# First loads of a two-layer decoder step reordered: x in quarters, params by GpSimd, first norm from row sums

## The chip, the core and the metric

The kernel runs as one launch on one core of a Trainium2 chip. The metric is device time in microseconds (us), the median of the runs. The engines are TensorE (PE in the rows; its weight loads are PEld), VectorE (DVE), ScalarE (ACT), GpSimd (POOL) and SyncE (SP); SP issues most of the DMAs, GpSimd and ScalarE can issue some too.

## What is computed

One inference step of a two-layer decoder trunk, in float32: 512 prompt rows and 8 x 4 sample rows of width 1024, so T = 544 rows together. The part that the change touches is the head of layer A:

```
h = rms(x, norm_mix[0])               # x * rsqrt(mean(x*x) + 1e-6) * gain
a, g, mq = split(h @ w_in_a[0], [768, 1536])
c, st = causal_dwconv(a * sigmoid(g), conv_a_prev, conv_a_w, conv_a_b)   # 31 taps
...
m = mem_attend(rms(mq), mem_k, mem_v)
x = x + concat([silu(layernorm(c)), m]) @ w_out_a
```

Behind it come a gated feed-forward part, a layer with differential attention over shared and paged keys and values, and a second feed-forward part. Twelve arrays are returned: the two results, and new states and caches.

## The kernel before, in words

Everything in the model's width is kept turned: channels on the 128 partitions, rows along the free axis. The residual `x_resid` is 128 x 8 x 544, eight chunks of 128 channels. Each engine has its own written-out program, and semaphores alone tie them together, so the order of every queue is the order of the code.

A product with a weight is a row of steps; one step is one block of 128 output channels. SP loads its slice of 512 KB (`w_raw`, four slots, `load`, L408). ScalarE rounds it to `w_hi` (`split_hi`, L990), VectorE makes the rest `w_lo` (`split_lo`, L1378), and the input is split in the same way into `xa_hi` (ScalarE, `scaled_hi`, L1020) and `xa_lo` (VectorE, `scaled_lo`, L1414), both with the norm's gain worked in. TensorE then runs, for each of the eight chunks k, hi times hi, lo times hi and hi times lo, each as two matmuls of 272 columns into two banks of `acc` (`mm_step`, L473): 48 matmuls a step. The norm's per-row factor `rstd` is multiplied in when VectorE takes the step's result out of `acc` (`from_acc`, L1446).

Steps 0 and 1 make the first 128 channels of a and of g (`glu_a`, `glu_g`). Before them stands the setup:

- SP (L390): constants, the x sample, the left half of x's columns, 16 loads of parameter rows and 4 small ones, the right half of x, then weight slices 0 and 1, conv states, FFN states, lambdas, memory rows, and the next slices.
- TensorE turns x and the parameter rows against an identity into two banks of `psT` in turn (L533 to L553), parameters between chunk 3 and chunk 4; VectorE copies each bank out (L1420 to L1429).
- ScalarE splits both weight slices and then, chunk by chunk, squares x (`square`, L1003) and makes `xa_hi`. GpSimd adds the squares up (`add_squares`, L2000), and there are two buffers of squares between them. TensorE sums over partitions with a matrix of ones after step 0 (`model_square_sum`, L501), VectorE turns, and takes the root with ScalarE (`root`, L1390), into `rstd`.
- Then a small part for the lambdas and the rest `tap_lo` of the conv's taps, `glu_a`, `glu_g`. Behind step 1 TensorE turns the memory rows and the states, sums their squares and goes on with step 2.

Of the conv's 31 taps ten a channel chunk run on TensorE as matmuls with diagonal matrices (`conv_unit`, L605), the others on VectorE.

Of the kernel before, what the change touches and what calls it, by code (L numbers as in the profile page):

```python
# [86 lines left out]
def build(nc, a):  # L87
    ctx = ExitStack()
    with ctx:
        def sem(name):  # L90
            return ctx.enter_context(nc.semaphore(name))
# [45 lines left out]
        small, _ = place("small", [P, 3, H * T // 32])  # L137
        lamt, _ = place("lam", [P, 8])
# [27 lines left out]
        frow, e1 = place("ffn_state_rows", [2 * 2 * DB, FF], at=e1)  # L166
        sprod, e2 = place("sample_tap_products", [P, DB, DS, TAPS], at=w0 + 12 * T)
# [59 lines left out]
        ld_x = [sem(f"ld_x{i}") for i in range(2)]  # L227
# [88 lines left out]
        SQ = dict(n0=0, mem=8, tA=16, ln=22, n1=28, n2=36, tB=44, n3=58)  # L316
        RT = dict(n0=0, mem=1, ln=2, n1=3, n2=4, n3=5)

        PARAMS_AT = KD // 2
# [44 lines left out]
        def tap_sum(j):  # L364
            return (psT, psX)[j % 2][:, :, 0:NPR // 2]
# [25 lines left out]
        def _(sp):  # L391
            sp.dma_start(cst[:, :], a["consts"]).then_inc(ld_const, 16)
            x_rows = a["x_prompt"].rearrange("o (i p) n -> (o p) i n", p=P)
            sp.dma_start(xnat[0:NSA, QB, :], a["x_sample"].rearrange("b t n -> (b t) n")).then_inc(ld_x[0], 16)
            sp.dma_start(xnat[:, 0:QB, 0:512], x_rows[:, :, 0:512]).then_inc(ld_x[0], 16)
            for r, k, src, done in put:
                if src is not None:
                    sp.dma_start(rows[r % P:r % P + k, r // P, :], src[done:done + k, :]).then_inc(ld_rows, 16)  # L398
                    continue
            for name in ("mem_q", "mem_k"):  # L400
                r = col[name]
                assert r // P == (r + 1) // P
                for h in range(2):
                    sp.dma_start(rows[r % P:r % P + 2, r // P, h * MHD:(h + 1) * MHD],
                                 a[name + "_norm"]).then_inc(ld_rows, 16)
            sp.dma_start(xnat[:, 0:QB, 512:D], x_rows[:, :, 512:D]).then_inc(ld_x[1], 16)
# [14 lines left out]
            for s in range(S_IN, S_MEM):  # L421
                m = s // 2 + CC * (s % 2) if s < 2 * CC else s
                load(s, block_cols(win, m))
                if s == 1:
                    sp.dma_start(crow[0:120, :, :], a["state_conv_a"][0].rearrange("(g b) t n -> (b t) g n", g=2)
                                 ).then_inc(ld_state, 16)
                    sp.dma_start(frow[:, :], a["state_ffn_conv"].rearrange("l b r n -> (l b r) n")).then_inc(ld_state, 16)
                    sp.dma_start(lamin[:, :, :].rearrange("p c n -> p (c n)"),
                                 a["lambdas"].rearrange("o c n -> o (c n)").partition_broadcast(P)).then_inc(ld_lam, 16)
# [42 lines left out]
        def _(pe):  # L472
# [62 lines left out]
            pe.wait_ge(ld_x[0], 32)  # L535
            b = setup_bank(0)
            for c in range(KD):
                last = nc.tensor.transpose(b[:, c * NSA:(c + 1) * NSA], xnat[0:NSA, QB, c * P:(c + 1) * P],
                                           ident[0:NSA, 0:NSA])
            last.then_inc(setup_filled, 1)  # L540
            for c in range(KD):
                if c == PARAMS_AT:
                    pe.wait_ge(ld_rows, 16 * (sum(1 for x in put if x[2] is not None) + 4))
                    b = setup_bank(1 + c)
# [4 lines left out]
                    pe.wait_ge(ld_x[1], 16)  # L549
                b = setup_bank(1 + c + (c >= PARAMS_AT))  # L550
# [1609 lines left out]
```

## Time and profile before

| | us |
|---|---|
| median of 3 runs | 1599.25 |
| lowest and highest run | 1593.43, 1603.15 |
| span of the profiled execution | 1595.4 |
| PE busy (matmul) | 1467.6 (92%) |
| DVE busy | 959.0 (60%) |
| ACT busy | 577.3 (36%) |
| POOL busy | 119.7 (8%) |

The page gives no time of the profiled execution beside its span. A busy PE is one with matmuls under way, pipelined, so 92% is no measure of how near it is to its peak. What a stretch costs is read from the chain of waits and from the timeline of that stretch, and not from shares of the whole span.

### The profile page before, as it was taken

The numbers are of one execution on the slowest core, as the hardware profiler recorded it, in microseconds if no ns is written. First come the engines' busy times: TensorE is split into PE (matmuls) and PEld (weight loads), VectorE is DVE, ScalarE is ACT, GpSimd is POOL, SyncE is SP. The second block draws the span as 40 slices with busy tenths as digits, with TensorE's granted clock in tenths as the row PEclk, the third lists the DMA queues.
The fourth block names the chain that finished last, engine by engine and source line by source line (L and its number), as shares of the span: only waits on it lengthen the run. The fifth ranks groups of instructions, "written<-read, shape, count | busy, mean of one in ns | idle before, by whom it ended". The sixth has DMA issues, their size and how long they took to land.

```text
span 1595.4 us, 27270 instructions
## 1 busy us (share of the span) xinstructions
PE 1467.6 (92%) x10820; PEld 1393.1 (87%) x10820; DVE 959.0 (60%) x1827; ACT 577.3 (36%) x949; POOL 119.7 (8%) x133
## 2 busy tenths in 40 slices
PE   4899867899999999999999996888999999999997
PEld 3799765789999999999888884765999999999997
DVE  4789888556663664466767775217366635653662
ACT  3444434444431222223445554125243322221232
POOL 2000103210000000001100003211010000000001
PEclk8899997789999999999999998998899999999999
DMA  7121222122233233222322224431123233233222
GB/s 208 42 65 54 93 79 81 30 66 82 85 87 93 85 87 93 81 85 74 91 73 60 68 65 167 165 104 53 40 80 93 80 92 93 80 93 88 85 74 67
DMA packets 208538, 134.87 MB, mean 85 GB/s; under 512 B 4971, under 2 KB 201152, under 8 KB 208391
## 3 DMA queue, kind: packets, MB, share of 16 engines
q1 hardware_dynamic: 201319, 105.30, 23.0%
q0 software_dynamic: 7120, 28.18, 5.4%
q8 instruction: 71, 1.16, 0.3%
q14 instruction: 28, 0.23, 0.0%
HBM read 126.24 MB, written 7.85 MB: 84 GB/s over the span
## 4 chain that ended last, share of the span: by engine, by line
PE 72%; DVE 17%; ACT 5%; issue 3%; DMA 1%; SPq 1%; POOL 0%; POOLq 0%; ACTq 0%; DVEq 0%
PE acc L485 55%; PE acc L662 6%; DVE conv_out L1478 3%; ACT w_hi L999 2%; PE acc L963 2%; DVE w_lo L1385 2%; PE psX L751 1%; PE psX L946 1%; DVE softmax_stats L1864 1%; ACT exps L1288 1%; DVE turned L1402 1%; DVE root_row L1411 1%; PE psT L696 1%; SPq L398 1%; PE psX L844 1%
## 5 line engine op out<-in xcount | busy, mean ns | idle before, releaser
L485 PE MATMUL acc<-xa_hi,w_hi 128*128 128x272 f32 x1824 | 384.8, 292 | 10.6 <-DVE xa_lo L1416 10.1
L485 PE MATMUL acc<-xa_hi,w_lo 128*128 128x272 f32 x1824 | 378.7, 289 | 0.0
L485 PE MATMUL acc<-xa_lo,w_hi 128*128 128x272 f32 x1824 | 377.6, 289 | 0.0
L999 ACT ACTIVATE w_hi<-w_raw 128x1024 fp32r<-128x1024 f32 x194 | 205.4, 1059 | 383.1 <-PE acc L485 306.5
L485 PEld LDWEIGHTS acc<-xa_hi,w_hi 128*128 128x128 f32 x1824 | 289.1, 189 | 13.1 <-issue 10.2
L1385 DVE TENSOR_TENSOR w_lo<-w_raw,w_hi 128x1024 fp32r<-128x1024 f32 x194 | 237.6, 1225 | 84.8 <-ACT w_hi L999 83.2
L485 PEld LDWEIGHTS acc<-xa_lo,w_hi 128*128 128x128 f32 x1824 | 288.3, 190 | 0.0
L485 PEld LDWEIGHTS acc<-xa_hi,w_lo 128*128 128x128 f32 x1824 | 286.2, 190 | 0.0
L485 PE MATMUL acc<-xb_hi,w_hi 128*128 128x272 f32 x832 | 174.8, 291 | 2.0 <-DVE xb_lo L1812 2.0
L485 PE MATMUL acc<-xb_hi,w_lo 128*128 128x272 f32 x832 | 172.1, 288 | 0.0
L485 PE MATMUL acc<-xb_lo,w_hi 128*128 128x272 f32 x832 | 171.6, 288 | 0.0
L1749 DVE TENSOR_TENSOR x_resid<-acc,x_resid 128x544 f32<-128x544 f32 (+1 forms) x64 | 46.4, 724 | 170.8 <-PE acc L485 139.9
L485 PEld LDWEIGHTS acc<-xb_hi,w_hi 128*128 128x128 f32 x832 | 130.6, 188 | 3.1 <-DVE xb_lo L1812 2.4
L485 PEld LDWEIGHTS acc<-xb_lo,w_hi 128*128 128x128 f32 x832 | 130.7, 188 | 0.0
L485 PEld LDWEIGHTS acc<-xb_hi,w_lo 128*128 128x128 f32 x832 | 129.9, 189 | 0.0
L1478 DVE SCALAR_TENSOR_TENSOR conv_out<-glu_ext,params,conv_out 128x512 f32<-128x512 f32 x120 | 86.2, 772 | 0.4
L1219 ACT ACTIVATE gelu<-gate_conv,params 128x544 f32<-128x544 f32 x44 | 33.0, 751 | 133.6 <-DVE gate_conv L1792 133.5
L1792 DVE SCALAR_TENSOR_TENSOR gate_conv<-gate_ext,params,gate_conv 128x512 f32<-128x512 f32 (+1 forms) x176 | 78.7, 497 | 0.1
L1803 DVE TENSOR_TENSOR value<-acc,rstd 128x544 f32<-128x544 f32 x44 | 31.9, 724 | 53.9 <-PE acc L485 53.9
L662 PE MATMUL acc<-xb_hi,w_hi 128*128 128x272 f32 x256 | 57.1, 306 | 7.6 <-DVE xb_lo L1741 5.7
L1223 ACT ACTIVATE xb_hi<-product 128x544 f32 x44 | 29.0, 658 | 89.1 <-DVE product L1809 89.1
L1812 DVE TENSOR_TENSOR xb_lo<-product,xb_hi 128x544 f32 (+1 forms) x44 | 31.9, 726 | 40.5 <-ACT xb_hi L1223 40.5
(298 smaller groups left out, 1989.3 us busy)
## 6 DMA issues: line engine op xcount, KB each, us to landing
w_raw<-in_w_up SPq DMA_DIRECT2D x88, 512.0 KB, 3.9
w_raw<-in_w_down SPq DMA_DIRECT2D x32, 512.0 KB, 3.9
w_raw<-in_w_in_a SPq DMA_DIRECT2D x14, 512.0 KB, 4.3
w_raw<-in_w_down SPq DMA_DIRECT2D x16, 384.0 KB, 3.3
w_raw<-in_w_kv SPq DMA_DIRECT2D x12, 512.0 KB, 3.8
k_pages<-in_cache_k POOLq DMA_DIRECT2D x16, 384.0 KB, 4.3
v_pages<-in_cache_v POOLq DMA_DIRECT2D x16, 384.0 KB, 3.9
w_raw<-in_w_mem_kv SPq DMA_DIRECT2D x8, 512.0 KB, 3.9
```

Source lines behind the costliest of these rows:

```text
L485: last = nc.tensor.matmul(acc[slot][:, c, 0:n], w, x[:, k, c * n:(c + 1) * n], start=(k == 0 and q == 0), stop=(k == kb - 1 and q == 2))
L662: last = nc.tensor.matmul(acc[s % 2][:, c, 0:HT], w, x[:, k, c * HT:(c + 1) * HT], start=(i == 0 and q == 0), stop=(i == KD - 1 and q == 2))
L963: last = nc.tensor.matmul(o_rows(h), apad[:, b2, pg, h, :], vpg[:, b2, pg, h * VD:(h + 1) * VD], start=(g + b2 + pg == 0 and h % 4 == 0), ...
L999: nc.scalar.activation(whi[:, slot % 2, :], wraw[:, slot, :], ACT.Copy).then_inc(w_hi_ready, 1)
L1219: nc.scalar.activation(gel[:, :], gcv[:, :], ACT.Gelu_apprx_tanh, bias=pcol_at("ffn_conv_b", q)).then_inc(gelu_ready, 1)
L1223: nc.scalar.activation(xb_hi[:, bass.ds(i * 2 + cc, 1), :].rearrange("p o n -> p (o n)"), prod[:, :], ACT.Copy).then_inc(uhi_ready, 1)
L1385: nc.vector.tensor_tensor(wlo[:, slot % 2, :], wraw[:, slot, :], whi[:, slot % 2, :].bitcast(F32), ALU.subtract).then_inc(w_lo_ready, 1)
L1478: ins = nc.vector.scalar_tensor_tensor(out=o, in0=src, scalar=w, in1=o, op0=ALU.mult, op1=ALU.add)
L1749: nc.vector.tensor_tensor(x, acc[b_][:, :, 0:HT], x, ALU.add).then_inc(acc_free, 1)
L1792: ins = nc.vector.scalar_tensor_tensor(out=o, in0=x, scalar=w, in1=o, op0=ALU.mult, op1=ALU.add)
L1803: nc.vector.tensor_tensor(val[:, :].rearrange("p (c n) -> p c n", c=2), acc[(sc + 1) % 2][:, :, 0:HT], rstd[:, :].rearrange("p (c n) -> p ...
L1812: nc.vector.tensor_tensor(lo, prod[:, :], hi.bitcast(F32), ALU.subtract).then_inc(ulo_ready, 1)
```

## The change

- SP loads only the identity's 128 columns of the constants first, then the x sample, the first quarter of x's columns, weight slice 0, the other three quarters of x, weight slice 1, and the other constants after that.
- GpSimd issues the parameter rows and the lambdas, ahead of its page table load and of its copy of the conv state from DRAM to DRAM.
- ScalarE issues one small load of the first norm's gains (`gain_rows`), which TensorE turns first of all.
- TensorE turns only the x sample and chunks 0 and 1 ahead of step 0; chunk k + 2 is turned between the matmuls of step 0, just before those of chunk k. The parameter rows are turned inside step 1, after chunk 5.
- VectorE's copies of chunks stand between its `xa_lo`, and ScalarE makes `xa_hi` as soon as a chunk is there.
- The first norm no longer comes from squares of the turned x that GpSimd adds. ScalarE squares the rows as loaded (128 rows x 1024, four and a short one) and sums along the row; VectorE makes variance, reciprocal root and five diagonal matrices, and TensorE multiplies ones by them, which spreads `rstd` over the partitions.
- A tap matmul on TensorE takes 512 columns into one bank, where there were two of 256 into two banks.

The core of the diff:

```diff
-            sp.dma_start(cst[:, :], a["consts"]).then_inc(ld_const, 16)
+            sp.dma_start(cst[:, 0:C_BLK], a["consts"][:, 0:C_BLK]).then_inc(ld_const, 16)
...
+            load_x(0)
...
                 load(s, block_cols(win, m))
+                if s == 0:
+                    for q in range(1, 4):
+                        load_x(q)
...
+            def x_arrives(k):
+                if k + 2 < KD:
+                    turn_x(k + 2)
+                pe.wait_ge(xg_lo, k + 1)
+
+            turn_x(0)
+            turn_x(1)
+            mm_step(0, 0, xa_hi, xa_lo, ready=x_arrives)
...
-            model_square_sum("n0")
-            mm_step(1, 1, xa_hi, xa_lo)
+            mm_step(1, 1, xa_hi, xa_lo, hooks=params_in)
+            for i in range(QB):
+                pe.wait_ge(n0_diag, i + 1)
+                nc.tensor.matmul(psX[:, 0, i * P:(i + 1) * P], ones[:, :], qf[:, 0, i * P:(i + 1) * P], start=True, stop=True)
...
-                    for c in range(2):
-                        at = PE_TAPS[i] + c * (NPR // 2)
-                        last = nc.tensor.matmul(tap_sum(j)[:, c, :], diag[:, u % 2, d, :], x[:, at:at + NPR // 2],
-                                                start=(i + q == 0), stop=(i == NPT - 1 and q == 2))
+                    last = nc.tensor.matmul(tap_sum(j), diag[:, u % 2, d, :], x[:, PE_TAPS[i]:PE_TAPS[i] + NPR],
+                                            start=(i + q == 0), stop=(i == NPT - 1 and q == 2))
...
+            act.dma_start(grow[:, :], a["norm_mix"].rearrange("l (c p) -> (l c) p", p=P)).then_inc(ld_gain, 16)
+            for c in range(KD):
+                act.wait_ge(setup_drained, c + 3)
+                scaled_hi(xa_hi, c, xT[:, c, :], pcol("norm_mix", c), xg_hi)
+                if c == 1:
+                    split_hi(0)
             split_hi(1)
-            for c in range(KD):
-                act.wait_ge(setup_drained, c + 2 + (c >= PARAMS_AT))
-                square(xT[:, c, :])
...
+                nc.scalar.activation(sqt[0:n, :, :].rearrange("p c n -> p (c n)")[:, 0:D], xnat[0:n, i, :], ACT.Square,
+                                     accum_out=rowsum[0:n, i:i + 1]).then_inc(n0_sum, 1)
...
+            for c in range(KD + 1):
+                if c < KD:
+                    dve.wait_ge(setup_filled, c + 3)
+                    nc.vector.tensor_copy(xT[:, c, 0:NPR], psT[:, c % 2, :]).then_inc(setup_drained, 1)
+                if c:
+                    scaled_lo(xa_lo, xa_hi, c - 1, xT[:, c - 1, :], pcol("norm_mix", c - 1), xg_hi, xg_lo, c)
+                if c == 1:
+                    split_lo(0)
             split_lo(1)
-            dve.wait_ge(sq_used, 8)
-            root(psX[:, :, 0:HT], T, 1.0 / D, EPS, rstd[:, :])
+            dve.wait_ge(setup_filled, 11)
+            nc.vector.tensor_copy(pT[:, 16:NROW], psT[:, 0, 16:NROW]).then_inc(setup_drained, 1)
...
+            for r, k, src, done in put:
+                if src is not None:
+                    pool.dma_start(rows[r % P:r % P + k, r // P, :], src[done:done + k, :]).then_inc(ld_rows, 16)
...
-            add_squares("n0")
```

How the instructions move, at the places that matter. TensorE before, from the last turns of x into step 0 (`psT` the banks for turning, `xa` the split input, `w` the split weights, `acc` the result; the name in brackets is the semaphore waited for):

```order
L547 MATMUL psT<-consts,param_rows 128x59
L552 MATMUL psT<-consts,x_rows 128x128 [waits setup_drained,ld_x1]
L552 MATMUL psT<-consts,x_rows 128x128 x3
...
L485 MATMUL acc<-xa_hi,w_hi 128x272 [waits xg_lo,w_lo_ready]
L485 MATMUL acc<-xa_hi,w_hi 128x272
L485 MATMUL acc<-xa_lo,w_hi 128x272 x2
L485 MATMUL acc<-xa_hi,w_lo 128x272 x2
L485 MATMUL acc<-xa_hi,w_hi 128x272 [waits xg_lo]
```

And TensorE after the change, at the same place:

```order
L551 MATMUL psT<-consts,x_rows 128x128 [waits setup_drained,ld_x0]
L551 MATMUL psT<-consts,x_rows 128x128 x3
L551 MATMUL psT<-consts,x_rows 128x128 [waits setup_drained,ld_x1,w_lo_ready]
L551 MATMUL psT<-consts,x_rows 128x128 x3
L487 MATMUL acc<-xa_hi,w_hi 128x272 [waits xg_lo]
L487 MATMUL acc<-xa_hi,w_hi 128x272
L487 MATMUL acc<-xa_lo,w_hi 128x272 x2
L487 MATMUL acc<-xa_hi,w_lo 128x272 x2
L551 MATMUL psT<-consts,x_rows 128x128 [waits setup_drained,ld_x1]
L551 MATMUL psT<-consts,x_rows 128x128 x3
```

The params' turn has gone from ahead of step 0 to inside step 1, and six of the eight chunk turns now stand between step 0's matmuls, the first of them behind the wait for the weights.

VectorE before, from the end of `xa_lo` to `glu_g`:

```order
L1416 SCALAR_TENSOR_TENSOR xa_lo<-x_resid,params,xa_hi 128x544 [waits xg_hi] x8
L1385 TENSOR_TENSOR w_lo<-w_raw,w_hi 128x1024 [waits w_hi_ready]
L1402 STREAM_TRANSPOSE turned<-psX 128x544 [waits sq_used]
L1404 TENSOR_SCALAR small<-turned 128x17 [waits turned]
L1409 RECIPROCAL small<-small 128x17 [waits sd_ready]
L1411 STREAM_TRANSPOSE rstd<-small 128x544 [waits dve_self]
L1440 TENSOR_TENSOR lambdas_in<-lambdas_in 128x64 [waits ld_lam,dve_self]
...
L1559 TENSOR_TENSOR tap_lo<-params,tap_hi 128x186 [waits taps_hi]
L1449 TENSOR_TENSOR glu_a<-acc,rstd 128x544 [waits mm_done,zeroed]
L1385 TENSOR_TENSOR w_lo<-w_raw,w_hi 128x1024 [waits w_hi_ready]
L1449 TENSOR_TENSOR glu_g<-acc,rstd 128x544 [waits mm_done]
```

And after the change:

```order
L1444 SCALAR_TENSOR_TENSOR xa_lo<-x_resid,params,xa_hi 128x544 [waits xg_hi] x2
L1413 TENSOR_TENSOR w_lo<-w_raw,w_hi 128x1024 [waits w_hi_ready]
L1463 COPY params<-psT 128x427 [waits setup_filled]
L1465 TENSOR_SCALAR small<-row_sums 128x5 [waits n0_summed]
L1468 RECIPROCAL small<-small 128x5 [waits n0_root]
L1472 TENSOR_SCALAR tile_raw<-consts,small 128x128 [waits dve_self]
L1472 TENSOR_SCALAR tile_raw<-consts,small 128x128 x3
L1472 TENSOR_SCALAR tile_raw<-consts,small 32x32
L1475 COPY rstd<-psX 128x512 [waits n0_rows]
L1476 COPY rstd<-psX 128x32
L1481 TENSOR_TENSOR lambdas_in<-lambdas_in 128x64 [waits ld_lam,n0_copied]
```

The copy of the params now stands ahead of the norm, behind it the diagonals and the wait for TensorE's rows; the lambdas, `tap_lo`, `glu_a`, `w_lo` and `glu_g` follow as before.

## Rows read from the trace of the kernel before

**Rows 1.** The profile page, its first line.

```profile
span 1595.4 us, 27270 instructions
```

**Rows 2.** Stretches: start:end, length, busy us of each engine (instructions), clock, DMA.

```profile
core 0: us, PE busy (x) PEld busy (x) DVE busy (x) ACT busy (x) POOL busy (x), PEclk, DMA share, GB/s
48.00:68.00 20.00, 15.01 (x69) 10.28 (x68) 12.65 (x25) 5.55 (x11) 0.00 (x0) 0.66 0.18 53
68.00:98.00 30.00, 29.40 (x238) 29.18 (x237) 27.42 (x50) 18.50 (x43) 0.00 (x0) 1.00 0.19 54
```

**Rows 3.** Chain that ended last, 0 to 70 us: start, length, what.

```profile
14.74 8.07 DMA w_raw<-in_w_in_a
...
30.04 6.90 DVE xa_lo L1416 x5
...
42.09 6.03 PE acc L485 x48
48.15 0.74 DVE glu_g L1449
```

**Rows 4.** DMA issues (KB each, us to landing), and one stretch's traffic.

```profile
x_rows<-in_x_prompt SPq DMA_DIRECT2D x1, 1024.0 KB, 10.1
out_s_conv_a<-in_state_conv_a POOLq DMA_DIRECT2D x1, 624.0 KB, 9.5
...
x_rows<-in_x_sample SPq DMA_DIRECT2D x1, 128.0 KB, 3.1
...
20.00:22.00 2.00, 1.30 (x9) 0.84 (x8) 1.85 (x4) 1.06 (x1) 0.00 (x0) 1.00 1.21 305
```

**Rows 5.** Timeline, TensorE: start, length, line, operation, count [idle before, releaser].

```profile
12.99 3.87 PE L552 MATMUL psT<-consts,x_rows 128*128 128x128 f32 x16
18.95 1.09 PE L552 MATMUL psT<-consts,x_rows 128*128 128x128 f32 x8 [1.01 <-DMA x_rows<-in_x_prompt]
30.97 0.79 PE L485 MATMUL acc<-xa_hi,w_hi 128*128 128x272 f32 x2 [9.33 <-DVE xa_lo L1416]
...
33.29 0.66 PE L485 MATMUL acc<-xa_lo,w_hi 128*128 128x272 f32 x2
33.74 0.66 PE L485 MATMUL acc<-xa_hi,w_lo 128*128 128x272 f32 x2
```

**Rows 6.** Timeline, VectorE: a copy, `w_lo`, `xa_lo` early and late, a small operation.

```profile
19.65 1.29 DVE L1429 COPY x_resid<-psT 128x512 f32<-128x512 f32 x2 [1.05 <-PE psT L552]
22.41 1.22 DVE L1385 TENSOR_TENSOR w_lo<-w_raw,w_hi 128x1024 fp32r<-128x1024 f32 x1
30.74 1.87 DVE L1416 SCALAR_TENSOR_TENSOR xa_lo<-x_resid,params,xa_hi 128x544 fp32r<-128x544 f32 x1
36.85 2.17 DVE L1416 SCALAR_TENSOR_TENSOR xa_lo<-x_resid,params,xa_hi 128x544 fp32r<-128x544 f32 x3
44.45 0.23 DVE L1440 TENSOR_TENSOR lambdas_in<-lambdas_in 128x64 f32<-128x64 f32 x1
```

**Rows 7.** Timeline, ScalarE: a weight's `w_hi`, five `xa_hi`, a table load.

```profile
20.74 1.06 ACT L999 ACTIVATE w_hi<-w_raw 128x1024 fp32r<-128x1024 f32 x1 [18.57 <-DMA w_raw<-in_w_in_a]
29.27 3.29 ACT L1021 ACTIVATE xa_hi<-x_resid,params 128x544 fp32r<-128x544 f32 x5
36.14 1.28 ACT L1018 ACT_TABLE_LOAD   x1
```

**Rows 8.** Timeline, GpSimd's adds and later DMA issues, and VectorE beside those.

```profile
33.19 3.17 POOL L2010 TENSOR_TENSOR square_total<-square_total,squares 128x544 f32<-128x544 f32 x2 [1.15 <-ACT squares L1008]
188.84 5.81 POOL L2019 DMA_DIRECT2D mem_cache<-in_cache_mem_k  x8
192.56 2.07 DVE L1478 SCALAR_TENSOR_TENSOR conv_out<-glu_ext,params,conv_out 128x512 f32<-128x512 f32 x3
```

**Rows 9.** Stretches, columns as in rows 2.

```profile
34.00:48.00 14.00, 13.21 (x95) 12.60 (x95) 10.98 (x17) 7.60 (x11) 2.21 (x2) 0.98 0.23 63
52.00:64.00 12.00, 10.18 (x48) 7.43 (x48) 8.55 (x21) 1.35 (x4) 0.00 (x0) 0.50 0.16 44
```

**Rows 10.** Chain that ended last: six tap matmuls in step 5.

```profile
86.12 0.71 PE psT L619 x6
```

More of the change, by code:

```diff
@@ L226, in build @@
         ld_const, ld_rows, ld_state, ld_mem = (sem(n) for n in ("ld_const", "ld_rows", "ld_state", "ld_mem"))
-        ld_x = [sem(f"ld_x{i}") for i in range(2)]
+        ld_x = [sem(f"ld_x{i}") for i in range(4)]
+        ld_gain, ld_xs, ld_masks = sem("ld_gain"), sem("ld_x_sample"), sem("ld_masks")
+        n0_sum, n0_var, n0_sd, n0_diag, n0_row, n0_done = (sem("n0_" + n) for n in (
+            "summed", "var", "root", "diagonals", "rows", "copied"))
         w_loaded = [sem(f"w_loaded{i}") for i in range(4)]
@@ L391, in _, with load_x @@
         def _(sp):
-            sp.dma_start(cst[:, :], a["consts"]).then_inc(ld_const, 16)
+            sp.dma_start(cst[:, 0:C_BLK], a["consts"][:, 0:C_BLK]).then_inc(ld_const, 16)
             x_rows = a["x_prompt"].rearrange("o (i p) n -> (o p) i n", p=P)
[L394 to L406, printed above, removed]
+            sp.dma_start(xnat[0:NSA, QB, :], a["x_sample"].rearrange("b t n -> (b t) n")).then_inc(ld_xs, 16)
+            def load_x(q):
+                cols = slice(q * (D // 4), (q + 1) * (D // 4))
+                sp.dma_start(xnat[:, 0:QB, cols], x_rows[:, :, cols]).then_inc(ld_x[q], 16)
+            load_x(0)
             def load(s, src, kb=KD):
@@ L540, in _, with turn_x @@
             last.then_inc(setup_filled, 1)
[L541 to L550 removed]
+            def turn_x(c):
+                pe.wait_ge(ld_x[c // 2], 16)
+                b = setup_bank(2 + c)
                 for i in range(QB):
@@ L555, in xa_ready, with params_in @@
                 return lambda k: pe.wait_ge(xg_lo, 8 * n + k + 1)
-            mm_step(0, 0, xa_hi, xa_lo, ready=xa_ready(0))
-            model_square_sum("n0")
-            mm_step(1, 1, xa_hi, xa_lo)
+            def x_arrives(k):
[5 more added lines that the diff above has]
+            mm_step(0, 0, xa_hi, xa_lo, ready=x_arrives)
+            def params_in(k):
+                if k == 5:
+                    pe.wait_ge(ld_rows, 16 * (sum(1 for x in put if x[2] is not None) + 4))
+                    b = setup_bank(10)
+                    for i in range(4):
+                        n = min(P, NROW - i * P)
+                        last = nc.tensor.transpose(b[:, i * P:i * P + n], rows[0:n, i, :], ident[0:n, 0:n])
+                    last.then_inc(setup_filled, 1)
+            mm_step(1, 1, xa_hi, xa_lo, hooks=params_in)
+            for i in range(QB):
+                pe.wait_ge(n0_diag, i + 1)
+                nc.tensor.matmul(psX[:, 0, i * P:(i + 1) * P], ones[:, :], qf[:, 0, i * P:(i + 1) * P], start=True, stop=True)
+            pe.wait_ge(n0_diag, QB + 1)
+            nc.tensor.matmul(psX[:, 1, 0:NSA], ones[0:NSA, :], qf[0:NSA, 0, NPR:T], start=True, stop=True).then_inc(n0_row, 1)
             pe.wait_ge(ld_mem, 16)
             for j in range(4):
-                b = setup_bank(10 + j)
+                b = setup_bank(11 + j)
                 for cc in range(2):
@@ new lines, in _ @@
+            settle()
+            for i in range(QB + 1):
+                n = P if i < QB else NSA
+                nc.vector.tensor_scalar(qf[0:n, 0, i * P:i * P + n], ident[0:n, 0:n], small[0:n, 2, i:i + 1], None, ALU.mult
+                                        ).then_inc(n0_diag, 1)
+            dve.wait_ge(n0_row, 1)
+            nc.vector.tensor_copy(rstd[:, 0:NPR], psX[:, 0, :]).then_inc(n0_done, 1)
+            nc.vector.tensor_copy(rstd[:, NPR:T], psX[:, 1, 0:NSA]).then_inc(n0_done, 1)
@@ L1439, in _ @@
+            dve.wait_ge(n0_done, 2)
             dve.wait_ge(ld_lam, 16)
```

96 lines of the change are left out of this document (52 added, 44 removed).

## The prediction

> **What bounds the kernel now.** I read three views in this order: the stretches of the program with each engine's busy time, the chain of waits that ended last, and the timeline of the first 50 us engine by engine. The span is 1595.4 us [rows 1]. From 68 us on TensorE is busy 29.40 of 30.00 us at a granted clock of 1.00; between 48 and 68 us it has 15.01 of 20.00 at 0.66 [rows 2]. The edit works ahead of both, so the place to read is the first 48 us, and the question is how much earlier the work that follows them can begin. I take the end of `glu_g` of step 1 as the mark: it is a piece of the chain (48.15 + 0.74 = 48.89 us), and the memory and state transposes behind it are the same on both sides [rows 3]. In the first 48 us the chain goes through the load of the second weight slice (14.74 to 22.81), ScalarE and GpSimd's squares, five `xa_lo` that take 6.90 us, then the matmuls of step 1 that end at 48.12 [rows 3].
>
> So three things make the head long. The first half of x lands 10.1 us after its issue, when GpSimd's copy of the conv state (9.5 us) lands too [rows 4]. The first weights are issued behind sixteen params loads, four small gain loads and all of x. And TensorE idles 9.33 us until `xa_lo` comes, which waits on ScalarE, which waits on the sum of squares [rows 5].
>
> **The change part by part.**
>
> *Loads.* Ahead of the second weight slice SP now issues 8 DMAs instead of 26. The bytes up to the first x quarter are 0.066 (identity), 0.131 (x sample) and 0.524 MB. At 305 GB/s [rows 4] from 2 us they have flowed by 4.4 us; with one more us to land I take 5.4. The x sample, issued just before, took 3.1 us from its issue [rows 4]: about 4.4 us again, and the gain row by ScalarE's queue at about the same time. Each further 0.52 MB costs 1.7 us: w0 7.1, x quarters 8.8, 10.5 and 12.2, w1 13.9. Both ends for the first quarter: 4.5 if it lands with its bytes, 12 if something holds it back as before.
>
> *First weights ready.* The clock is low at first: 16 transposes took 3.87 us against 8 in 1.09 us later [rows 5]; less the last one's tail I take 0.86 us and 0.44 us for a chunk of four. From 4.4 us the x sample's eight small turns take about 1.0 (half of a large one each), chunks 0 and 1 0.86 each, and with 0.4 of hand-overs all are done by 7.5 us. A copy is 0.65 us, `w_hi` 1.06, `w_lo` 1.22 [rows 6, 7]. VectorE's order is copy, copy, `xa_lo`, `w_lo`; ScalarE's two `xa_hi` (0.66 each) and `w_hi`. That puts `w_lo` of step 0 at 11.1 us. Then chunk 2 is turned, and the first matmul runs at 12.0 instead of 30.97 [rows 5]: **18.95 us gained**.
>
> *Step 0.* Per chunk TensorE now turns a chunk and runs six matmuls. At half clock two matmuls start every 0.45 us (33.29, 33.74 [rows 5]), so 1.37 + 0.86 = 2.23 us; at full clock 0.75 (48 in 6.03 [rows 3]) + 0.44. VectorE needs a copy and an `xa_lo`. The latter took 1.87 us beside GpSimd's adds and 2.17/3 = 0.72 without [rows 6, 8]; the adds are gone, so about 1.42 us a chunk with a hop. Before, the clock was full from 34 us, three after the first matmul [rows 5, 9]; here TensorE is dense from 11.1, and I take it to be full from 16. Chunks 0 and 1 at half clock, chunk 2 in between, the rest on VectorE: it ends at 24.1. `w_lo` of step 1 follows at 24.8.
>
> *Step 1.* 6.0 us, and the params' turn (0.5) inside: its end is 31.5. From first matmul to there 19.5 us, where before it was 48.12 - 30.97 = 17.15: **2.3 us given back**.
>
> *First norm.* Before, rstd came under step 1, and 0.77 us after step 1's end `glu_g` was done. Now params turn at 30.1 and are copied by 30.8. ScalarE's five squares of 1024 elements, like `w_hi` 1.06 each, run 23.6 to 29.2, then a table load of 1.28 [rows 7]: 30.5, about level. Variance, root, reciprocal and five small diagonals at some 0.22 each [rows 6] end at 32.9; five matmuls and two copies give rstd at 34.3. The lambda steps and `tap_lo` stand there as before (to 36.2); then `glu_a` 0.72, `w_lo` 1.22, `glu_g` 0.72: 38.9. That is 7.4 us behind step 1's end instead of 0.77: **6.6 us given back**. Those five diagonal matmuls and copies are new; I bound them by 0.2 and 0.7 us each and keep the middle.
>
> Sum: 18.95 - 2.3 - 6.6 = **10.0 us**, so 48.89 becomes 38.9.
>
> *Params through GpSimd.* Twenty-one DMAs at 0.73 us (8 in 5.81 [rows 8]) from 1.2 us are issued by 16.5 and landed by about 20; PE wants them at 29. The cover is 9 us. If it is gone, the waiting params turn holds the rest of step 1 on TensorE, VectorE's copy and the whole norm behind it, and ScalarE's root, `tap_hi` and the weights of step 2. Here the Trainium skill speaks against the change. In the trace those eight issues ran back to back beside a VectorE at work on conv taps (three in 2.07 us) [rows 8]. "SBUF — State Buffer", section "SBUF: two separate sides", says that a DMA from GpSimd cannot write its descriptors while VectorE holds the shared port pair, and gives 620 ns alone against about 3100 ns beside a VectorE copy, an estimate of 65 us for all 21, and with params landing then a kernel some 30 us slower. By the row it is 16.5 us and costs nothing. The trace agrees with the row's short time, but shows no copy out of PSUM beside an issue, so the rule stays as a rival.
>
> The displaced loads (conv-state copy behind the params, masks, states, memory rows, w2, w3) have some 8 MB to move by 35 us at about 300 GB/s: 27 us. Nothing is late. SP loses issue time that only it waited for.
>
> *Tap matmuls.* Six of 256 columns take 0.71 us [rows 10], six of 272 0.75. Per column that leaves about 0.23 us for one of 512: 0.69 instead of 0.71, over 60 units at most 1.2 us, least 0. VectorE's conv taps are on the chain there, so I take nothing.
>
> Nothing after 68 us waits for a fixed time, so the shift reaches the end: 1595.4 - 10.0 = 1585.4. The page gives no time for the profiled execution beyond its span; the median of the runs is 3.9 us above it, so 1599.25 - 10.0 = **1589.2**. About 0.5%, 8 us, can be told from no change.
>
> **The rivals.**
>
> *The clock stays low through steps 0 and 1.* Step 0 then runs at 2.23 a chunk (end 27.7), step 1's 48 matmuls at 0.225 (10.9 us): params turned at 37, `glu_g` at 45.7, a gain of 3.2, **1596**. Against it: transposes alone brought 0.24 us each down to 0.136 between 17 and 19 us [rows 5]. For it: between 52 and 64 us TensorE was busy 10.18 of 12 us, mostly with transposes, at 0.50 [rows 9]. "TensorE: Matmul & The Clock Gate", section "Part 4: PE-mode transpose", says that transposes do not count as busy in the same way. By that rule alone the mix here would stay slow; the trace shows it both ways. But over half of TensorE's time here goes to true matmuls, behind which the clock rose before.
>
> *The first quarter is held back.* If the load order does not do what it says, and x lands at 12 again because w0, the quarters and GpSimd's small loads share the DMA engines, 5.4 us are left: **1594**. Against it: the long tail before is the conv-state copy's, and that now starts after 16 us.
>
> *Slower: params too late.* If each GpSimd issue that falls beside VectorE's work waits out a whole chunk (2.2 us) before its own 0.73, the 14 after 6.5 us end at 47.6 and land at 51: `glu_g` at 60, **1610**. It decides from a landing later than 39 us on. Against it stand the eight issues [rows 8]. This is the port rule of "SBUF — State Buffer" above, priced from rows.
>
> *More.* With the clock up at the first matmul and rstd's new pieces at their lower bounds, the gain is 14: **1585**.
>
> **How the numbers follow.** Forecast 0.58 (6 to 12 us gained), clock 0.18, held back 0.08, too late 0.04, more 0.12. The likeliest gives 1587 to 1593; the first two rivals and the spread of the runs shown (1593 to 1603) widen it to 1581 to 1598. Faster by over 0.5% asks for a gain of 8 us: most of the forecast, all of "more", none of the others: 0.62. Slower takes only the late params: 0.04. The rest, 0.34, is no change that can be told.
>
> **What would show it.** First matmul of step 0 near 12 us; `xa_lo` at 0.7 us each; step 0 over by 24 to 25; the params' turn not waiting on a DMA; rstd near 34; `glu_g` near 39; from there each piece 10 us earlier. A step 0 past 27 means the clock; a TensorE wait on the params rows means GpSimd; a `glu_g` at 39 with no shorter span would mean that the head never set the end.

## The result and the profile after

The changed kernel takes 1585.79 us (median of five runs, 1582.49 to 1587.74) against 1599.1 us for the kernel before on the same chip: ratio 0.9925, 95% interval 0.9903 to 0.9946, that is 9 to 16 us. The forecast was 1589.2 us, a gain of 10. The profiled execution is 11.8 us shorter than the one of before [rows 1]:

```profile
span 1583.6 us, 26914 instructions
```

The first place to look is the queues. These rows of the timeline are SyncE's issues and GpSimd's (start, length of the issue, engine, line, what, count):

```profile
1.82 0.41 SPq L404 DMA_DIRECT2D x_rows<-in_x_prompt  x1
2.28 0.51 SPq L413 DMA_DIRECT2D w_raw<-in_w_in_a  x1
2.83 2.84 SPq L404 DMA_DIRECT2D x_rows<-in_x_prompt  x3
5.71 1.39 SPq L413 DMA_DIRECT2D w_raw<-in_w_in_a  x1
...
6.76 1.03 POOL L2040 DMA_DIRECT2D param_rows<-in_ffn_conv_w  x2
7.78 0.53 POOL L2040 DMA_DIRECT2D param_rows<-in_ffn_conv_b  x1
8.30 0.51 POOL L2040 DMA_DIRECT2D param_rows<-in_k_norm  x1
```

The second weight slice goes out at 5.71 us, where before it went out at 14.74 [rows 3]. GpSimd's 21 issues follow each other at 0.5 to 0.6 us (the first took 0.69). The timeline of TensorE and VectorE shows what comes of it:

```profile
5.93 1.97 PE L551 MATMUL psT<-consts,x_rows 128*128 128x128 f32 x8 [0.92 <-DMA x_rows<-in_x_prompt]
12.45 0.80 PE L487 MATMUL acc<-xa_hi,w_hi 128*128 128x272 f32 x2
16.13 0.60 PE L551 MATMUL psT<-consts,x_rows 128*128 128x128 f32 x4
24.74 0.52 PE L487 MATMUL acc<-xa_hi,w_hi 128*128 128x272 f32 x2 [0.37 <-DVE w_lo L1413]
29.35 0.69 PE L572 MATMUL psT<-consts,param_rows 128*128 128x128 f32 x4
...
7.09 0.69 DVE L1456 COPY x_resid<-psT 128x512 f32<-128x512 f32 x1 [1.61 <-PE psT L551]
7.94 0.69 DVE L1456 COPY x_resid<-psT 128x512 f32<-128x512 f32 x1 [0.16 <-PE psT L551]
10.40 1.23 DVE L1413 TENSOR_TENSOR w_lo<-w_raw,w_hi 128x1024 fp32r<-128x1024 f32 x1 [1.02 <-ACT w_hi L1019]
20.32 0.78 DVE L1444 SCALAR_TENSOR_TENSOR xa_lo<-x_resid,params,xa_hi 128x544 fp32r<-128x544 f32 x1
23.46 1.23 DVE L1413 TENSOR_TENSOR w_lo<-w_raw,w_hi 128x1024 fp32r<-128x1024 f32 x1 [0.17 <-ACT w_hi L1019]
```

The first matmul of step 0 stands at 12.45 us instead of 30.97 [rows 5]. An `xa_lo` takes 0.78 us with GpSimd's adds gone, where it took 1.87 beside them [rows 6]. Four transposes take 1.97/2 us at 5.93 and 0.60 at 16.13: TensorE has gone from half to full rate between them. And the params' turn at 29.35 has no idle time noted ahead of it, so it waits for no load.

The chain of waits shows the part that the change gives back, from step 1 to `glu_g`:

```profile
24.74 4.77 PE acc L487 x36
29.51 0.53 PE psT L572 x4
30.04 1.70 PE acc L487 x12
31.74 1.02 PE psX L578 x8
...
35.48 0.72 DVE glu_a L1490
36.20 1.18 DVE w_lo L1413
37.38 0.64 DVE glu_g L1490
```

Step 1 ends at 31.74 us, `glu_g` at 38.02: 6.3 us in which TensorE does the norm's five small matmuls (ten rows of the trace, 8 and 2) and the first eight memory turns. Before, the distance was 0.77 us. So `glu_g` is done 10.9 us earlier (48.89 before by the chain [rows 3]; the table below has 48.87, from VectorE's timeline).

Behind it the stretches (columns as in [rows 2]) show TensorE idle and its clock down, as they did before [rows 9]:

```profile
34.00:38.00 4.00, 0.12 (x2) 0.00 (x0) 3.45 (x8) 2.68 (x4) 0.00 (x0) 0.82 0.01 2
38.00:42.00 4.00, 0.00 (x0) 0.00 (x0) 2.26 (x6) 1.60 (x2) 0.00 (x0) 0.50 0.44 132
46.00:50.00 4.00, 3.80 (x25) 2.65 (x24) 2.33 (x7) 0.00 (x0) 0.00 (x0) 0.50 0.00 0
```

From 70 to about 210 us every piece comes 11.3 us earlier, to within 0.4. From there the two traces drift: 8.8 us at 306, 8.4 at 1022, 11.8 from 1089 to the end. The code of those stretches is the same on both sides (the last tap matmul stands at 210.8 us in the kernel before). In the stretch where most of the drift back falls the granted clock differs, as these rows of before and, 8.4 us earlier, of after show:

```profile
1020.00:1040.00 20.00, 17.20 (x101) 13.34 (x100) 4.62 (x17) 4.47 (x9) 3.76 (x7) 0.91 0.40 138
```

```profile
1011.60:1031.60 20.00, 17.75 (x110) 13.92 (x109) 4.62 (x17) 4.48 (x9) 4.06 (x8) 1.00 0.47 155
```

That the clock makes the drift is read from such pairs and was not tried by itself. Hence the yardstick for the runs below is the end of `glu_g` of step 1; the total adds some 3 us either way from later stretches. It is a fair yardstick as long as what stands behind `glu_g` stays as it is; the last two kernels change that too, and are also read at 89 us.

### The profile page after: what moved, and what is told of

It is laid out like the page before. It is cut to its first block, busy times and chain, and to the rows that moved or that the text cites. A ratio compares the mean times of both kernels' runs of the same rounds, so it can differ in the third digit from the quotient of the medians.

```text
span 1583.6 us, 26914 instructions
## 1 busy us (share of the span) xinstructions
PE 1465.3 (93%) x10643; PEld 1383.9 (87%) x10643; DVE 956.6 (60%) x1833; ACT 578.9 (37%) x951; POOL 122.0 (8%) x149
## 4 chain that ended last, share of the span: by engine, by line
PE 72%; DVE 17%; ACT 5%; issue 3%; DMA 1%; POOLq 0%; POOL 0%; ACTq 0%; SPq 0%; DVEq 0%
PE acc L487 55%; PE acc L682 6%; DVE conv_out L1519 4%; DVE w_lo L1413 2%; ACT w_hi L1019 2%; PE acc L983 2%; PE psX L771 1%; DVE softmax_stats L1905 1%; ACT exps L1316 1%; PE psX L966 1%; DVE turned L1430 1%; DVE root_row L1439 1%; PE psT L716 1%; PE psX L639 1%; PE psX L864 1%
```

## The experiments

Ten more kernels were measured. This table has the end of `glu_g` of step 1, its gain on before, and the time against the kernel before of the same session.

| kernel | `glu_g` ends, us | gained there | total: median, ratio to before (95%) |
|---|---|---|---|
| before | 48.87 | | |
| changed kernel | 38.02 | 10.9 | 1585.79, 0.9925 (0.9903 to 0.9946) |
| new loads alone | 43.25 | 5.6 | 1592.6, 0.9970 (0.9955 to 0.9985) |
| new loads and gain row | 40.66 | 8.2 | 1588.67, 0.9952 (0.9938 to 0.9966) |
| state copy later | 45.40 | 3.5 | 1594.28, 0.9984 (0.9972 to 0.9996) |
| changed, params on SyncE | 45.02 | 3.9 | 1591.52, 0.9966 (0.9955 to 0.9978) |
| changed, turns first | 38.42 | 10.5 | 1584.9, 0.9925 (0.9901 to 0.9950) |
| changed, taps of 256 | 38.23 | 10.6 | 1583.82, 0.9909 (0.9889 to 0.9929) |
| changed, params late | 46.58 | 2.3 | 1594.75, 0.9975 (0.9960 to 0.9990) |
| changed, extra matmuls | 38.52 | 10.4 | 1584.82, 0.9908 (0.9889 to 0.9928) |
| short tail | 35.32 | 13.6 | 1579.34, 0.9896 (0.9870 to 0.9921) |
| short tail, memory early | 36.47 | 12.4 | 1578.14, 0.9876 (0.9860 to 0.9893) |

**New loads alone.** The kernel before with SyncE's and GpSimd's new order of loads; all that computes stays.

```
-  sp.dma_start(cst[:, :], a["consts"])
+  sp.dma_start(cst[:, 0:C_BLK], a["consts"][:, 0:C_BLK])
   sp.dma_start(xnat[0:NSA, QB, :], ...)
-  sp.dma_start(xnat[:, 0:QB, 0:512], ...)       (first half of x)
-  for r, k, src, done in put: sp.dma_start(rows...)
-  sp.dma_start(xnat[:, 0:QB, 512:D], ...)
+  load_x(0)             (quarters 1 to 3 behind the weights of step 0)
...
+  for r, k, src, done in put: pool.dma_start(rows...)
```

> The kernel before with the new load order alone (identity, x sample, x in quarters around the first weights, params and lambdas by GpSimd, masks later); turns, sum of squares and first norm stay as they were. My theory: in the kernel before the first matmul of step 0 (30.97 us) hung on the chain w1 landing (22.81) - ScalarE's second w_hi - squares - xa_hi - xa_lo, and VectorE's GpSimd-crowded xa_lo of 1.87 us each stay. With w1 landing at about 16.1 us that chain moves by 6.7 us: first matmul near 24.3, end of glu_g of step 1 near 42.2, total about 6.5 us under the kernel before. The loads then give the larger part of the 11 us and the new order of turns and norm some 4. Rival A (the order of turns and the norm from row sums are what gains, the loads only make it possible): first matmul still past 28, under 3 us gained. Rival B (the loads give it all): 10 us or more gained.

The first matmul came at 25.76 us and `glu_g` at 43.25: 5.6 us gained against 6.7 expected. The size was near, the reason was not. The chain, read from its start:

```profile
1.46 8.28 POOL param_rows L1996 x16
9.74 1.49 POOL param_rows L2001 x3
11.23 6.61 DMA param_rows<-in_mem_k_norm
...
17.88 1.19 PE psT L544 x4
19.07 1.90 PE psT L549 x8
```

Not the second weights (landed at 14.93) but the last params row, 17.84 us, released TensorE: in this kernel the params are turned between the halves of x, and the gain of `xa_hi` comes out of them. The changed kernel loads that gain by itself, a small row on ScalarE's queue. I had counted it as a detail. The next run adds it.

**New loads and the gain row.** As above, the gain row loaded and turned with the x sample, the params turned between steps 0 and 1.

```
+  act.dma_start(grow[:, :], a["norm_mix"]...).then_inc(ld_gain, 16)
-      if c == PARAMS_AT: (turn of the params)
...
+  nc.vector.tensor_copy(pT[:, 0:16], psT[:, 0, KD * NSA:KD * NSA + 16])
   mm_step(0, 0, ...); model_square_sum("n0")
+  (turn of the params)
   mm_step(1, 1, xa_hi, xa_lo)
```

> The kernel before with the new load order as in the loads-only kernel, and besides the gain row of the first norm by ScalarE's queue, turned with the x sample, and the params turned between steps 0 and 1 instead of between the halves of x. Turns ahead of step 0, sum of squares by GpSimd and the old norm stay. In the loads-only kernel the first matmul hung on the last params row (17.84 us), because xa_hi takes its gains from the params. Theory: without that the first xa_lo comes at about 18 us, step 0 then paces with VectorE's xa_lo of 1.87 us beside GpSimd's adds and ends near 30 to 31, step 1 at 37 to 38, and glu_g, 0.77 us behind it as in the kernel before, at 38.5 to 40: 9 to 10 of the 10.9 us that the change gained come without the new order of turns and without row sums, total 8 to 10 us under the kernel before. Rival: row sums and the new turns are worth the rest, glu_g at 42 or later, total under 6.5 us below the kernel before.

`glu_g` ended at 40.66 us: 8.2 us gained, between the theory (9 to 10) and its rival. Rows of its timeline and, first, of its chain:

```profile
5.61 9.57 DMA w_raw<-in_w_in_a
...
18.41 0.79 PE L483 MATMUL acc<-xa_hi,w_hi 128*128 128x272 f32 x2 [3.90 <-DVE xa_lo L1416]
20.91 9.20 DVE L1416 SCALAR_TENSOR_TENSOR xa_lo<-x_resid,params,xa_hi 128x544 fp32r<-128x544 f32 x6 [0.84 <-ACT xa_hi L1021]
```

Now the second weights are what the chain begins with. The first matmul is at 18.41, six us later than in the changed kernel, and step 0 with its sum of squares is long: `xa_lo` takes 1.53 us on average (9.20/6) beside GpSimd's adds. The granted clock, too, read 0.50 from 20 to 28 us, behind the 3.90 us that TensorE had stood idle; in the changed kernel it is full from 16. But the old norm runs under step 1, so at `glu_g` only 2.6 us of those six are left. Loads and gain row, with the params' turn behind step 0, are worth three quarters of the gain. The other 2.6 belong to the rest of the change: the turns between the matmuls, the row sums, and ScalarE's new order. In this kernel ScalarE splits the second weights, landed at 15.18, before the first `xa_hi`; in the changed one it does so after the last.

**Turns first.** The changed kernel with all eight turns of x ahead of step 0.

```
-  turn_x(0)
-  turn_x(1)
+  for c in range(KD):
+      turn_x(c)
...
-      if k + 2 < KD:
-          turn_x(k + 2)
```

> The changed kernel with all eight x turns ahead of step 0 instead of between its matmuls. My theory: the turns wait for the last quarter (13.68 us), VectorE's copies and xa_lo run per chunk as they come, so the first matmul comes near 16 to 17.5 us instead of 12.45; the matmuls then run without waiting for VectorE, at the full clock because it has risen meanwhile (48 in 6.03 us): step 0 ends near 23.5 against 24.4, and the total is within 1 us of the changed kernel: VectorE sets the end of step 0 either way and the interleaving itself is worth nothing. Rival (interleaving gains): if the clock is still at half when the matmuls begin, they take 10.9 us, step 0 ends at 27 to 28, and the total is 3 to 4 us above the changed kernel.

```profile
17.52 0.80 PE L487 MATMUL acc<-xa_hi,w_hi 128*128 128x272 f32 x2
...
20.39 0.65 PE L487 MATMUL acc<-xa_hi,w_hi 128*128 128x272 f32 x2
20.84 0.56 PE L487 MATMUL acc<-xa_lo,w_hi 128*128 128x272 f32 x2
```

The first matmul came five us later than in the changed kernel, `glu_g` 0.4 us later, the total the same: the size is as the theory had it, the way is not. The clock was still at half (the pairs start 0.45 us apart until 21.24, 0.25 from there), so TensorE itself paced step 0, without a gap, to 25.25 instead of the 23.5 expected. Step 1 then followed at once, its `w_lo` done three us before, where the changed kernel ends step 0 at 24.4 and waits 0.37 us for that `w_lo`. With the run above this leaves the turns 0.4 us and, by subtraction, about 2.2 for the row sums, the orders of ScalarE and VectorE and the clock together. None of these was tried alone, so how the 2.2 divide stays open.

**Params on SyncE.** The changed kernel with its params issued by SyncE behind the first x quarter.

```
   load_x(0)
+  for r, k, src, done in put: sp.dma_start(rows...)
+  for name in ("mem_q", "mem_k"): ... sp.dma_start(rows...)
...
-  (the same loops on pool)
```

> The changed kernel with its params rows back on SyncE, between the first x quarter and the first weights (lambdas with the weights of step 1); all else as changed. My theory: SyncE issues some 20 small loads at about 0.58 us each before w0, so w0 lands near 19 to 20 us instead of 8.1; w_lo of step 0 near 22 to 23, first matmul near 23 to 24 instead of 12.45, and all behind it later by the same, less what TensorE's clock and the turns of the further quarters make up: glu_g of step 1 at 46 to 49 instead of 38.0, total 8 to 11 us above the changed kernel, that is, no gain over the kernel before. Rival (what counts is the interleaving and the row sums, the weights have slack): at most 3 us above the changed kernel.

The chain has SyncE's issues from 2.28 us one behind the other, the first weights at 12.23, landing at 16.35:

```profile
4.81 3.13 SPq L409
...
12.23 4.12 DMA w_raw<-in_w_in_a
```

First matmul 19.51 (expected 23 to 24, since the weights landed earlier than thought), `glu_g` 45.02, seven us above the changed kernel; expected 8 to 11. The rival (at most 3) is out: without the new queue for the small loads two thirds of the gain at `glu_g` are gone. But this run changes two things. GpSimd, with no params to issue, starts its copy of the conv state at 2.18 us instead of 13.06, and one small issue, at 4.81, took 3.13 us where the others took 0.25 to 0.5. The first weights went out 9.95 us later than in the changed kernel: some 7 of these are the small loads at their usual pace, and nearly 3 are that one issue, which may be the copy's doing (next run). The two were not separated.

**State copy later.** The kernel before with GpSimd's copy of the conv state behind its adds.

```
-  pool.dma_start(a["s_conv_a"]..., a["state_conv_a"]...)
...
+  pool.dma_start(a["s_conv_a"]..., a["state_conv_a"]...)    (behind the adds)
```

> The kernel before with GpSimd's copy of the conv state issued behind its adds of squares instead of first. It tests whether that copy held back the first half of x (10.1 us from its issue, landing together with the copy). My theory: the copy was the tail: the first half of x lands near 7 instead of about 12 us, but the first matmul of step 0 stays near 31, since it hangs on w1 and the sum of squares: total within 0.5 us of the kernel before. Rival A (x's landing was on the path): 4 to 5 us gained. Rival B (the bytes ahead of it hold x back, not the copy): x lands at 11 to 12 as before, no gain.

Neither theory nor rivals: 3.5 us gained at `glu_g`, 27.51 instead of 30.97 for the first matmul. The copy did hold back the first half of x (7.4 us from its issue instead of 10.1), but what set the end was SyncE. One row of its queue before, and the same row of this run:

```profile
6.22 3.92 SPq L398 DMA_DIRECT2D param_rows<-in_conv_a_w  x3
```

```profile
5.97 1.06 SPq L398 DMA_DIRECT2D param_rows<-in_conv_a_w  x3
```

The same three small issues took 3.92 us beside the copy and 1.06 without. So the second weights went out at 11.21 instead of 14.74 [rows 3], landed at 19.34 instead of 22.81, and the head moved by just that:

```profile
11.21 8.13 DMA w_raw<-in_w_in_a
```

My theory had taken the issue times of SyncE for fixed. In the changed kernel the copy starts at 13.06 (with the new loads alone at 12.98), behind all that is urgent; part of the gain of both is this.

**Taps of 256.** The changed kernel with each tap matmul in two halves again.

```
-  last = nc.tensor.matmul(tap_sum(j), ..., x[:, PE_TAPS[i]:PE_TAPS[i] + NPR], ...)
+  for c in range(2):
+      at = PE_TAPS[i] + c * (NPR // 2)
+      last = nc.tensor.matmul(tap_sum(j)[:, c, :], ..., x[:, at:at + NPR // 2], ...)
```

> The changed kernel with each tap matmul of 512 columns split into two of 256 again, as before the change. My theory: it costs nothing that can be seen: total within 1.2 us of the changed kernel, head unchanged (glu_g of step 1 near 38.0), a unit of taps 0.71 us against about 0.69. Rival (the merged taps give part of the 11.8 us that the span lost, mostly late in the program): 2 us or more above the changed kernel, and the shift against the kernel before falls between 70 and 285 us, where the conv units run.

1583.82 us against the changed kernel's 1585.79, each with its own session's before: no cost that can be told, as expected, and the rival (2 us or more) is out. On the chain a unit takes 0.70 to 0.73 us here and 0.68 to 0.70 in the changed kernel.

**Params late.** The changed kernel with 38 chained writes of an idle buffer ahead of the params on GpSimd.

```
+  for i in range(38):
+      pool.memset(total[:, :], 0.0).then_inc(held, 1)
+      pool.wait_ge(held, i + 1)
   for r, k, src, done in put:
```

> The changed kernel with 38 chained writes of an idle GpSimd buffer ahead of the params loads, estimated at some 0.5 to 0.6 us each, so that the params land about 21 us later, near 39 to 40 instead of 18.5. My theory: params are wanted by TensorE at 29.35 inside step 1, so the cover is some 11 us; past it every us counts: the turn waits about 10 us with the rest of step 1, the norm and tap_hi behind it, glu_g of step 1 ends near 48 instead of 38.0 and the total is 9 to 10 us above the changed kernel, less if the landing is earlier (landing time minus 29.35, less some 1 us). Rival (the head does not end on the params' path, other work covers it, as the mem turns behind): under 3 us.

The params landed at 35.82 us, earlier than planned (the last load came down within 1.6 us of its issue). TensorE waited, and then was slow:

```profile
35.86 1.19 PE L573 MATMUL psT<-consts,param_rows 128*128 128x128 f32 x4 [6.11 <-DMA param_rows<-in_mem_k_norm]
...
37.06 3.02 PE acc L488 x12
```

The formula put the loss for this landing at 5.5 us; `glu_g` ended 8.56 us later. The turn starts 6.35 us later (29.51 to 35.86, by the chains). The rest is the clock: the turn took 1.19 us instead of 0.53, the 12 matmuls behind it 3.02 instead of 1.70, the norm's eight 1.25 instead of 1.02; together that is the 8.56. The granted clock read 0.50 from 36 to 40 us. So past the cover it costs us for us, and two more for the clock behind the idle time. The rival "params too late" has its mechanism and more than its price; the landing it needs did not come.

**Extra matmuls.** The changed kernel with eight matmuls, results unused, in TensorE's idle time behind the norm.

```
+  if j == 2:
+      pe.wait_ge(n0_done, 2)
+      for c in range(8):
+          nc.tensor.matmul(psX[:, 0, :], ones[:, :], xT[:, c, 0:NPR], start=True, stop=True)
   b = setup_bank(11 + j)
```

> The changed kernel with 8 more fp32 matmuls of 272 columns, whose results are not used, on TensorE in its idle time behind the norm's matmuls (about 34 to 42 us). In the changed kernel the granted clock falls to 0.50 from about 37 us and stays until about 53, over the mem and state transposes. Theory: the idle time costs the clock; with TensorE busy to 40 us the transposes at 42.6 begin at the full clock, six of them take 0.8 instead of 1.6 us, step 2 begins 2 to 4 us earlier and the total is 2 to 4 us below the changed kernel. Rival: the stretch waits on VectorE's copies or on loads, not on TensorE's pace: total within 1 us. Second rival: mere idle time is not what lowers the clock, transposes do, and the clock still reads 0.50 between 42 and 53 us.

```profile
34.00:38.00 4.00, 4.00 (x14) 2.00 (x13) 3.41 (x10) 2.68 (x4) 0.00 (x0) 1.00 0.00 0
38.00:42.00 4.00, 3.60 (x9) 1.33 (x7) 2.33 (x4) 1.60 (x2) 0.00 (x0) 1.00 0.46 131
42.00:46.00 4.00, 2.46 (x14) 1.44 (x14) 3.65 (x10) 0.72 (x2) 0.00 (x0) 1.00 0.45 131
46.00:50.00 4.00, 3.82 (x29) 3.16 (x30) 2.47 (x9) 0.00 (x0) 0.00 (x0) 0.72 0.01 4
50.00:54.00 4.00, 4.00 (x10) 2.30 (x9) 3.67 (x7) 1.66 (x4) 0.00 (x0) 0.50 0.01 2
```

The matmuls have 512 columns each, where the expectation says 272, and keep TensorE busy from 34.47 to 41.60 us. The clock held at 1.00 to 46 us; in the changed kernel, idle there, it stood at 0.50 from 38 us on. But it fell all the same while TensorE, busy 3.82 of 4 us, ran the small transposes of the states, and of the memory norm's matmuls (6.6 us) most ran at half. Step 2 began half a us earlier (56.26 against 56.73), and the total is the same, as the first rival had it: the next turns wait for VectorE's copy either way, to 43.11 us here and 42.61 in the changed kernel. So the clock fell once behind idle time and once in transposes, and a gain of 2 to 4 us is not to be had this way. "TensorE: Matmul & The Clock Gate" of the Trainium skill, "Part 4: PE-mode transpose", says that the full clock does not engage for transposes. This run agrees; the next one does not, nor do the transposes of [rows 5], which sped up with no matmul ahead of them.

**Short tail.** The changed kernel, with what stood between rstd and `glu_g` done earlier: params turned behind chunk 1 of step 1, lambda steps, `tap_hi` and `tap_lo` in the idle time ahead of the norm, `glu_g` ahead of the `w_lo` of step 2.

```
-          if k == 5:      (turn of the params in step 1)
+          if k == 1:
...
+  (lambda steps, tap_lo on VectorE here)
   dve.wait_ge(n0_sum, QB + 1)
...
   from_acc(s, atile[:, :]).then_inc(acc_free, 1)
-  split_lo(s + 2)
+  if s: split_lo(s + 2)
...
   from_acc(s, gtile[:, :]).then_inc(acc_free, 1)
+  if s == 1: split_lo(2)
```

> The changed kernel with the params turned after chunk 1 of step 1 instead of chunk 5, and what stands between rstd and glu_g on VectorE moved into its idle time ahead of the norm (lambda steps, tap_hi and tap_lo), and glu_g ahead of the w_lo of step 2. Theory: the norm's path is squares (29.20), table load (30.5), root, diagonals, matmuls, rstd at 33.9, unchanged; then glu_a and glu_g at once: glu_g ends near 35.4 instead of 38.0, w_lo of step 2 as late as before or earlier, and the total is 2 to 3 us below the changed kernel. Rival: TensorE's next work waits on something else (the clock, w_lo of step 2, loads landing at 27 to 31 us): glu_g early but the total within 1 us.

Chain, and the next row of TensorE's timeline:

```profile
33.97 0.72 DVE glu_a L1495
34.69 0.64 DVE glu_g L1495
...
39.92 1.97 PE L586 MATMUL psT<-consts,mem_rows 128*128 128x128 f32 x8 [5.79 <-DVE mem_t L1643]
```

`glu_g` ends at 35.32, 2.7 us earlier. So 2.7 of the 5.5 us that the first norm gave back were an order of work, not work. The total went to 1579.34, more than the 2 to 3 us expected. Step 2 begins at 52.49 us instead of 56.38, and at 89 us the pieces come 15.2 us before those of the kernel before, where the changed kernel had 11.3: 1.2 us more are gained behind `glu_g`. There the stretches (columns as in [rows 2]) have the clock rise again while TensorE runs only transposes, to 46.6 us:

```profile
38.00:42.00 4.00, 2.06 (x9) 1.69 (x10) 3.16 (x8) 0.72 (x2) 0.00 (x0) 0.50 0.86 247
42.00:46.00 4.00, 3.46 (x26) 2.27 (x27) 2.84 (x7) 0.00 (x0) 0.00 (x0) 0.83 0.00 1
```

In the changed kernel it stayed at 0.50 through these transposes; why it rose here is open.

**Short tail, memory early.** Besides, VectorE's copies of the turned memory and states ahead of the weight remainders of steps 2 and 3, which take TensorE's 5.79 us wait away.

```
   dve.wait_ge(n0_done, 2)
+  (copies of the first two memory banks)
...
   from_acc(s, gtile[:, :]).then_inc(acc_free, 1)
+  if s == 1: (the other two, the conv and ffn states)
   split_lo(2)
```

> The kernel with the short tail, and besides VectorE's copies of the turned memory and states moved ahead of the weight remainders of steps 2 and 3 and of glu_ext (the first two copies ahead of glu_a). In the kernel with the short tail TensorE stands idle from about 34 to 39.92 us, until the first of these copies frees its banks. Theory: that idle time is VectorE's order alone, the mem turns go on at about 35 us, step 2 begins near 48.5 instead of 52.5, and the total is 3 to 4 us below the kernel with the short tail. Rival: the clock (0.50 in that stretch) or the weight remainders that are now later hold step 2, and under 1.5 us is gained.

```profile
34.67 1.25 PE L586 MATMUL psT<-consts,mem_rows 128*128 128x128 f32 x8 [0.58 <-DVE mem_t L1492]
```

The wait is 0.58 us and the following pieces come 18.0 us before those of the kernel before at 89 us, where the short tail alone had 15.2. Step 2 begins at 48.40, as the theory had it (48.5). By 216 us 1.7 of the 18.0 is lost, in a stretch where the granted clock read 0.71 (in before 0.87). Its median is 1578.14 us; against the short tail's 1579.34, each measured in its own session, the two cannot be told apart, so of the 3 to 4 us expected the total shows at most the rival's 1.5. This kernel beats both of the pair: its interval, 0.9860 to 0.9893, lies below the changed kernel's 0.9903 to 0.9946. The short tail's (0.9870 to 0.9921) lies below 1 but overlaps with it.

## Why the prediction was right

By its own steps, predicted and measured:

| step | predicted, us | measured |
|---|---|---|
| first x quarter landed | 5.4 | 5.9 |
| first, second weights landed | 7.1, 13.9 | 8.1, 16.1 |
| `w_lo` of step 0 | 11.1 | 11.6 |
| first matmul of step 0 | 12.0 | 12.45 |
| clock full from | 16 | 16.1 |
| step 0 ends | 24.1 | 24.4 |
| step 1 ends | 31.5 | 31.7 |
| rstd | 34.3 | 33.9 |
| `glu_g` ends | 38.9 | 38.0 |
| gained there | 10.0 | 10.9 |

- **First matmul:** 18.5 us gained instead of 18.95. The loads come somewhat slower than the 305 GB/s of [rows 4] gave; the second weights are 2.2 us later than worked out, without effect, since ScalarE turns to them only at 22.4.
- **Step 0** takes 1.30 to 1.73 us a chunk for VectorE's copy, `xa_lo` and hops once the clock is up, where 1.42 was taken; the adds' price of [rows 6] is gone. VectorE is not alone on the path: from 16 us on the chain goes back and forth between its copies and `xa_lo` and TensorE's matmuls and turns, and VectorE waits 0.34 and 0.26 us for turned chunks.
- **The clock** rose where the sum put it; the rival with half rate through step 1 is out. Here the mix of turns and matmuls did bring the full clock.
- **The norm** is where the 0.9 us lie: from the params' copy to the last diagonal 1.6 us instead of 2.1, the matmuls and copies behind 1.65 instead of 1.4, from `tap_lo` to `glu_g` 2.5 instead of 2.7. From step 1's end 6.3 us against 7.4 in the sum, so 5.5 given back instead of 6.6. The table load ended at 30.49, as worked out, with some luck: the squares began 0.3 us early and came 1.18 us apart instead of some 1.1, since each is followed by a read of its sum. The path is another one than in the sum, too: the last diagonal was ready at 32.27, and the chain goes through TensorE, which comes to the norm's matmuls only when step 1 ends, at 31.74.
- **GpSimd's issues** took 0.5 us, the last params row landed at 18.51. The issues at 6.76 to 8.81 ran straight through two VectorE copies out of PSUM (7.09 to 8.64), so the rival's wait is not there. "SBUF — State Buffer" of the Trainium skill, "SBUF: two separate sides", ties the block to VectorE operations in a two-port mode, such as an fp32 copy from SBUF to SBUF. None of the copies beside these issues is of that kind: the prediction had carried the rule over to them, and this run does not test it.
- **The taps** cost and gained nothing that one run could tell.
- **The held-back quarter** did not happen; the conv-state copy that held x before also held SyncE's issues, which the prediction had not seen and did not need.
- **Slips in the working**, none of which moves the result: ahead of the second weights stand 7 issues instead of 25 (8 and 26 count the weights themselves); step 1's terms, 24.8 + 6.0 + 0.5, end at 31.3 and not 31.5; the loads listed as displaced come to some 4 MB, and the 8 MB are all that moves in the first 36 us. For the quarter held back, 6.6 us off the 10.0 leave 3.4, and the working doesn't show how 5.4 were left.

So the mechanism held step by step; that the sum came within 0.9 us owes something to errors in both directions. The measured median gain, 13.3 us, is above the 10.9 of `glu_g`. The profiled pair has 11.3 from the head, and the rest from later stretches whose clock differs between executions; what of the 13.3 is noise can't be told, with an interval of 9 to 16 us.

## What to carry to other kernels

Read a slow start as a race of queues: count what stands ahead of the first weights on each queue, and move what is wanted late (params, state copies) to another queue and behind. When a norm or reduction is taken out of the matmuls' way, see where its tail comes to stand: here 5.5 us of it came back, 2.7 of which another order of the same instructions saves. An early first matmul is worth only what reaches the end of the next step: five us of it were worth 0.4 here.

## What the runs showed of the hardware

- A DRAM-to-DRAM copy on GpSimd's queue lengthened SyncE's issues, by one pair of traces: three small ones took 3.92 us beside it, 1.06 without. It isn't the only thing that does: in the changed kernel one issue at 7.14 took 2.71 us, before that copy began at 13.06.
- GpSimd issued 21 loads at 0.5 to 0.6 us each beside VectorE's copies out of PSUM; the eight of [rows 8] took 0.73 each.
- The clock column reads 1.00 over the first 34 us of the changed kernel, yet transposes and matmuls there run at half rate until about 16 us (0.45 us from one pair of matmuls to the next, then 0.25). In the kernel before it reads 1.00 to 24 us, over the slow transposes at 12.99 [rows 5] too. In the first stretch the pace of the rows, not that column, tells the clock.
- Six us of idle TensorE in step 1 brought its next matmuls down to half rate (12 in 3.02 us instead of 1.70, at a granted clock of 0.50).
- VectorE's `xa_lo` took 1.87 us beside GpSimd's adds [rows 6] and 0.78 without them.
